# A hybrid decoder layer: moved waits at the stage borders, and head norms summed in fp32r on split squares

## The reference, cut to what matters

```python
def _rmsnorm(x, g):
    y = xf * lax.rsqrt(jnp.mean(xf * xf, axis=-1, keepdims=True) + EPS)
    return (y * g.astype(jnp.float32)).astype(x.dtype)
...
x = x + 0.5 * _swiglu(_rmsnorm(x, ffn1_norm[l]), ffn1_w_gu[l], ffn1_w_down[l])
h = _rmsnorm(x, mix_norm[l])
proj = h @ w_in[l]                       # q,k,v (stick-breaking), q,k,v (dilated), q (memory), gates
o_sb = _stick_breaking(q_sb, k_sb, v_sb)                 # 6 heads of 64
qd = _rmsnorm(q_d.reshape(B, S, N_DIL_HEADS, HEAD_DIM), dil_q_gain[l]) * scale
kd = _rmsnorm(k_d.reshape(B, S, N_DIL_HEADS, HEAD_DIM), dil_k_gain[l])
o_dil = _dilated_attention(qd, kd, v_d, rel_bias)
o_x = _memory_attention(qx, mk, mv)                      # 4 heads, 256 memory tokens
merged = g0 * (o_sb @ w_br_sb) + g1 * (o_dil @ w_br_dil) + g2 * (o_x @ w_br_x)
x = x + merged @ w_out[l]
x = x + 0.5 * _swiglu(_rmsnorm(x, ffn2_norm[l]), ffn2_w_gu[l], ffn2_w_down[l])
```

## Time and profile before

| | |
|---|---|
| three runs, median | 2374.99 us (2374.26 to 2375.61) |
| the profiled execution | 2375.41 us, span of the trace 2373.6 us |
| TensorE busy | 2331.7 us (98%) |
| VectorE busy | 1127.6 us (48%) |
| ScalarE busy | 612.1 us (26%) |
| GpSimd busy | 66.0 us (3%) |
| mean granted clock of TensorE | 0.995 |

### The profile page before, as it was taken

The page is one execution under the profiler, slowest core; times in us unless marked ns, Lnnn a source line. Parts: engine busy times, 40 slices in busy tenths (PEclk is TensorE's granted clock), DMA queues, the critical chain, the costliest instruction groups (busy, mean ns, idle before and its releaser), DMA issues.

```text
span 2373.6 us, 25801 instructions
## 1 busy us (share of the span) xinstructions
PE 2331.7 (98%) x10664; PEld 1869.5 (79%) x10664; DVE 1127.6 (48%) x1118; ACT 612.1 (26%) x787; POOL 66.0 (3%) x47
## 2 busy tenths in 40 slices
PE   8999999999999999989999999999999999999998
PEld 6888888888887766667677888878888888888887
DVE  8443444344346567755535333355444444444334
ACT  6211111111113567745344111133111111111111
POOL 2000000000002000010000000011000000000000
PEclk9999999999999999999999999999999999999999
DMA  5211111111111300110122111131111111111112
GB/s 159 75 45 53 44 53 36 53 53 44 53 47 57 115 18 18 27 42 30 29 26 63 54 45 54 54 115 37 62 51 47 51 46 49 40 53 49 49 53 71
DMA packets 47424, 125.78 MB, mean 53 GB/s; under 512 B 4285, under 2 KB 20829, under 8 KB 47104
## 3 DMA queue, kind: packets, MB, share of 16 engines
q1 hardware_dynamic: 45776, 112.69, 15.7%
q10 hardware_dynamic: 624, 10.03, 1.1%
q0 software_dynamic: 960, 2.15, 0.5%
HBM read 116.42 MB, written 9.87 MB: 53 GB/s over the span
## 4 chain that ended last, share of the span: by engine, by line
PE 92%; DVE 5%; ACT 2%; issue 1%; DMA 0%; SPq 0%; ACTq 0%; DVEq 0%
PE ps L1434 90%; DVE h_lo L920 1%; DVE w_lo L913 0%; PE ps L1914 0%; PE ps L1849 0%; DVE d_qk L1036 0%; DVE xT L982 0%; DVE x_p L1161 0%; PE ps L2005 0%; DVE pr_x L1057 0%; DMA x_nat<-in_x 0%; DVE d_qk L1060 0%; ACT pr_x L649 0%; DVE xT L1097 0%; DVE h_lo L1360 0%
## 5 line engine op out<-in xcount | busy, mean ns | idle before, releaser
L1434 PE MATMUL ps<-h_hi,w_hi 128*128 128x512 f32 x2240 | 879.5, 397 | 6.1 <-ACT h_hi L876 2.1
L1434 PE MATMUL ps<-h_lo,w_hi 128*128 128x512 f32 x2240 | 863.5, 390 | 0.2 <-DVE h_lo L920 0.2
L1434 PE MATMUL ps<-h_hi,w_lo 128*128 128x512 f32 x2240 | 701.0, 390 | 0.0
L1434 PEld LDWEIGHTS ps<-h_hi,w_hi 128*128 128x128 f32 x2240 | 420.8, 188 | 128.0 <-issue 38.9
L1434 PEld LDWEIGHTS ps<-h_hi,w_lo 128*128 128x128 f32 x2240 | 421.6, 188 | 89.6 <-DVE w_lo L913 0.4
L1434 PEld LDWEIGHTS ps<-h_lo,w_hi 128*128 128x128 f32 x2240 | 421.6, 188 | 86.8 <-issue 1.9
L576 ACT ACTIVATE w_hi<-raw 128x1024 fp32r<-128x1024 f32 x196 | 204.2, 1051 | 797.3 <-PE ps L1434 778.4
L913 DVE TENSOR_TENSOR w_lo<-raw,w_hi 128x1024 fp32r<-128x1024 f32 x196 | 249.2, 1279 | 159.6 <-ACT w_hi L576 150.1
L982 DVE TENSOR_TENSOR xT<-xT,ps 128x1024 f32<-128x1024 f32 x175 | 213.4, 1219 | 179.7 <-PE ps L1434 179.7
L1434 PE MATMUL ps<-a_hi,w_hi 128*128 128x512 f32 x704 | 275.7, 392 | 5.7 <-DVE w_lo L913 4.9
L1434 PE MATMUL ps<-a_lo,w_hi 128*128 128x512 f32 x704 | 274.7, 390 | 0.0
(11 more groups left out here) (199 smaller groups left out, 1512.9 us busy)
## 6 DMA issues: line engine op xcount, KB each, us to landing
raw<-in_weights SPq DMA_DIRECT2D x196, 512.0 KB, 3.5
x_nat<-in_x SPq DMA_DIRECT2D x8, 512.0 KB, 7.4
...
```

Of the source, the lines that this page charges most:

```text
L1434: return pe.matmul(o, a, b, start=start, stop=stop, skip_group_check=True)
```

## The change

At the start, x tile 0 is loaded, transposed and split in two halves of 512 positions, and the loads of the identity, the gains and the bias table go to other queues. Before stick-breaking, projection 6 goes to its own PSUM pair and the first scores are issued ahead of the transposes of v. In the late steps `xq_scale` follows `beside_copy`, and the scores of memory quarter 0 follow the last `sb_within`. In the memory stage the head sum of the six norm projections is made in four fp32r products of a rounded square `sq_hi` (ScalarE) and a rest `sq_lo` (GpSimd), behind two more product rows of the projection; `x_divide` is made one round earlier; on ScalarE "keep" is separated from `proj_rstd`, with `x_exp` between. Ahead of dilated attention the first scores and a fill go before the last transposes. Several PSUM pairs are exchanged.

```diff
 def proj_pair(n):
-    return 2 if n < PR_SB else n % 2 if n < PR_DIL else 2 + (n - PR_DIL) % 2
+    return 2 if n < PR_SB else n - PR_SB if n < PR_SB + 2 else 3 if n < PR_DIL else 2 + (n - PR_DIL) % 2
...
         def _(sp):
-            sp.dma_start(rel[0:32, :], rel_bias).then_inc(rel_in, 16)
-            sp.dma_start(ident, consts[:, 0, :]).then_inc(ident_in, 16)
-            sp.dma_start(g_raw[:], gains).then_inc(gain_in, 16)
-            for k in range(DT):
+            sp.dma_start(x_nat[:, 0, 0:4], x[0:512, 0:P].rearrange("(b p) c -> p b c", p=P)).then_inc(x0_in, 16)
+            sp.dma_start(raw[:, 0, :], weights[0]).then_inc(raw_in[0], 16)
+            sp.dma_start(x_nat[:, 0, 4:8], x[512:S, 0:P].rearrange("(b p) c -> p b c", p=P)).then_inc(x_in[0], 16)
+            for k in range(1, DT):
...
+            def square_split(i):
+
+                pool.wait_ge(pr_sq_done, 2 + i + 1)
+                pool.wait_ge(pr_sq_hi_done, i + 1)
+                nc.gpsimd.tensor_tensor(sq_lo[:], pr_x[0][:], sq_hi[:].bitcast(F32), ALU.subtract).then_inc(pr_sq_split, 1)
...
                     nc.scalar.activation(pr_sq[:, 0:w], proj_dest(n), ACT.Square).then_inc(pr_sq_done, 1)
+                    if n >= PR_DIL:
+                        nc.scalar.activation(sq_hi[:], proj_dest(n), ACT.Square).then_inc(pr_sq_hi_done, 1)
...
                 if n:
-                    proj_rstd(p - 1)
+                    proj_keep(p - 1)
                 if n + 1 < 8:
                     x_exp(n + 1)
+                if n:
+                    proj_rstd(p - 1)
...
-                if xq_at(s - 1) is not None:
-                    xq_scale(xq_at(s - 1))
...
                 if half_done(s) is not None:
                     beside_copy(half_done(s))
+                if xq_at(s - 1) in (0, 1, 2):
+                    xq_scale(xq_at(s - 1))
...
                 if n < 8:
-                    x_divide(n)
-                if n < 8:
                     split_lo(proj_unit(p) + AHEAD)
+                if n == 0:
+                    xq_scale(3)
                 if n + 1 < 8:
                     x_lowest(n + 1)
-                if n:
+                    x_divide(n + 1)
+                if 0 < n < 8:
                     proj_final(p - 1)
...
+                if kind == "norm" and n >= PR_DIL:
+                    pe.wait_ge(head_ready, 1)
+                    pe.wait_ge(pr_sq_split, kept_before(n) + 1)
+                    for c in (0, 512):
+                        mm(ps[:, to, c:c + 512], head_r[:], sq_hi[:, c:c + 512], True, False)
+                        last = mm(ps[:, to, c:c + 512], head_r[:], sq_lo[:, c:c + 512], False, True)
+                    last.then_inc(pr_aux, 1)
+                    return
...
-                beside(s, early, 4)
-                if s + 1 == SB_STEPS:
-
-                    pe.wait_ge(xq_final, 1)
-                    pe.wait_ge(xq_kept, 4)
-                    x_scores(0)
+                if s:
+                    beside(s, early, 4)
+                else:
+                    pe.wait_ge(pr_final, aux_before(PR_DIL))
                 sb_within(s)
+            pe.wait_ge(xq_kept, 4)
+            x_scores(0)
+            v_turn(2 * BESIDE - 1)
...
+                proj(PR_DIL + n, hh, hl, k0=DT // 2, k1=DT - 2)
                 if n:
                     proj_aux(PR_DIL + n - 1)
-                if n < 7:
-                    proj(PR_DIL + n, hh, hl, k0=DT // 2)
-                    x_values(n)
-                else:
-                    proj(PR_DIL + n, hh, hl, k0=DT // 2, k1=DT - 2)
-                    x_values(n)
-                    proj(PR_DIL + n, hh, hl, k0=DT - 2)
-
-            pe.wait_ge(xa_o, 8)
+                x_values(n)
+                proj(PR_DIL + n, hh, hl, k0=DT - 2)
+
+            pe.wait_ge(xa_exp, 32)
             pe.wait_ge(pr_final, aux_before(PR_DIL + 6))
             d_scores(0)
-            proj_aux(PR_DIL + 7)
...
-            pe.wait_ge(pr_final, aux_before(len(PROJ)))
+            pe.wait_ge(pr_final, aux_before(PR_DIL + 7))
+            fill(0)
+            proj_aux(PR_DIL + 7)
+            pe.wait_ge(xa_o, 8)
             for n in range(DN):
```

More of the change, by code:

```diff
@@ L276, in layer @@
         pr_x = [at(f"pr_x{i}", AR + (56 + 4 * i) * K, [P, S]) for i in range(3)]
+        sq_hi, sq_lo = at("sq_hi", AR + 12 * K, [P, S], F32R), at("sq_lo", AR + 56 * K, [P, S], F32R)
+        head_r = at("head_r", AR + 32 * K, [P, P], F32R)
         o_sb = at("o_sb", AR, [P, 3, S])
@@ L550, in _ @@
                     pool.dma_start(bias[:, hh, c:c + w], src).then_inc(bias_in[hh], 16)
+            for i in range(6):
+                square_split(i)
             pool.wait_ge(d_exp, DN // 2)
@@ L813, in _ @@
                 p = PR_DIL + n
+                if n == 1:
+                    act.wait_ge(xq_final, 4)
                 if n:
@@ L1271, in _ @@
                     beside_copy(half_done(s))
+                if xq_at(s - 1) in (0, 1, 2):
+                    xq_scale(xq_at(s - 1))
             sb_add(SB_STEPS - 1)
             x_lowest(0)
+            dve.wait_ge(sb_z, SB_STEPS)
+            nc.vector.tensor_copy(head_r[:], head_ones).then_inc(head_ready, 1)
             v_out(2 * BESIDE - 1)
+            x_divide(0)
             sb_out(SB_STEPS - 1)
@@ L1423, in _ @@
                     dve.wait_ge(unit_done, U_OUT + m + 1)
-                nc.vector.tensor_tensor(xT[:, m, :], x_back[:, m, :], ps[:, 2 + m % 2, :], ALU.add).then_inc(x_added, 1)
+                nc.vector.tensor_tensor(xT[:, m, :], x_back[:, m, :], ps[:, 3 - m % 2, :], ALU.add).then_inc(x_added, 1)
             for k in range(5, DT):
@@ L1593, in proj @@
                     if n < PR_DIL:
-                        after(pe, pr_copied, n if n < PR_SB else n - 1)
+                        if n == PR_DIL - 1:
+                            pe.wait_ge(newton, 4)
+                        else:
+                            after(pe, pr_copied, n if n < PR_SB else n - 1)
                     else:
@@ L1628, in proj_aux @@
                     last.then_inc(pr_aux, 1)
-            def projections(n0, n1, hi, lo):
-                for n in range(n0, n1):
-                    proj(n, hi, lo)
-                    if n == n0:
-                        norm_sum(1)
-                    else:
-                        proj_aux(n - 1)
-                proj_aux(n1 - 1)
             def turn_x(k):
@@ L1648, in _ @@
             pe.wait_ge(ident_in, 16)
-            turn_x(0)
-            turn_x(1)
+            pe.wait_ge(x0_in, 16)
+            for b in range(4):
+                last = pe.transpose(ps[:, 2, b * P:(b + 1) * P], x_nat[:, 0, b, :], ident)
+            last.then_inc(x0_turned, 1)
+            pe.wait_ge(x_in[0], 16)
+            for b in range(4, 8):
+                last = pe.transpose(ps[:, 2, b * P:(b + 1) * P], x_nat[:, 0, b, :], ident)
+            last.then_inc(x_turned, 1)
+            pe.wait_ge(hi_done, 1)
+            pe.wait_ge(h0_hi_done, 1)
+            mm(ps[:, 0, 0:512], w_hi[:, 0, 0, :], h_hi[:, 0, 0:512], True, False)
             for k in range(DT):
@@ L1818, in _ @@
             pe.wait_ge(tri_ready, 3)
+            pe.wait_ge(pr_copied, PR_SB + 2)
             sb_scores(0)
             sb_scores(1)
+            proj_aux(PR_SB + 2)
+            beside(0, 0, 4)
             for s in range(SB_STEPS):
@@ L1925, in d_values @@
                         r = head * HD
-                        last = mm(ps[r:r + HD, 2, i * P:(i + 1) * P], v_dil(g)[:, kb, r:r + HD],
+                        last = mm(ps[r:r + HD, 3, i * P:(i + 1) * P], v_dil(g)[:, kb, r:r + HD],
                                   d_pT[:, (n + head) % 3, j * P:(j + 1) * P], j == 0, j == len(held) - 1)
@@ L1991, in _ @@
                 if m == 0:
-                    last = streamed(2, u % NW, mg_hi_done, mg_split, 0)
+                    last = streamed(3, u % NW, mg_hi_done, mg_split, 0)
                 else:
-                    last = product(2 + m % 2, u % NW, hh, hl, S, read=out_read if m == DT - 1 else None)
+                    last = product(3 - m % 2, u % NW, hh, hl, S, read=out_read if m == DT - 1 else None)
                 last.then_inc(unit_done, 1)
```

59 lines of the change are left out of this document (39 added, 20 removed).

## The result

The changed kernel takes 2387.8 us (median of five runs, 2386.5 to 2390.7), the kernel before 2374.3 us on the same chip. The ratio is 1.0056, with a 95% interval of 1.0044 to 1.0068: slower by 13.5 us, where 2369.4, 5 us faster, was forecast. The profiled execution took 2390.7 us, with a span of 2388.9; it is the longest of the five and lies 2.9 above the median.

The account below looks back on a forecast made before the run. The prediction took TensorE (98% busy) to bound nearly everything. Its terms summed to +6.0 us gained, so 2375.4 - 6.0 = 2369.4 us, with a range of 2363 to 2376.

Parts of the forecast that it names:

- start: At the kernel's start, x loaded first in its queue could bring tile 0's transposes ahead; little gained, +0.3 us.
- ahead of stick-breaking: Between projection 6 and stick-breaking, first scores and beside(0) fill TensorE's waits, with a new wait of 1.0; +5.2 us.
- late stick-breaking and into memory: Late steps: xq_scale behind beside_copy delays sb_values, -1.5 us; entering memory attention: two waits go, two product rows come, +0.8.
- rest of stage: Memory stage after the last head sum: products, the sum and a wait no longer fall in it; +4.3 us.
- into dilated attention: Entry to dilated attention: first scores and a fill cover the copy, at full clock; +7.6 us, +3.2 if the clock falls.
- all behind it: Behind the entry to dilated attention: merge_pair and the output pairs change no work; 0.
- the six sums: Memory stage: the chain through GpSimd's subtraction binds, five rounds take 91.2 us in place of 83.0; -8.2 us.
- clock in this stage: Memory stage: the clock falls at three of five TensorE waits at the sum, 0.8 us each; -2.5 us.
- Rival B: Memory stage: the clock falls at all five waits, 6.2 us in place of 2.5; 2374 us, no change; chance 0.16.
- rival C: Memory stage: a clock fall lasts after each of five waits, TensorE's round of 20.5 binds; 2382 us, slower; chance 0.09.

Follow-up runs that it names:

- the o_x experiment: Changed kernel with VectorE's o_x copy put right behind x_divide, ahead of proj_final: 2372.6 us, ratio 0.9989 to the kernel before.
- the three edits: Changed kernel with o_x copy ahead of proj_final, tile 1 turned ahead of the first product, and xq_scale ahead of beside_copy: 2367.7 us, ratio 0.9972 to before.
- the sum ahead: Changed kernel with the head sum put back ahead of the two product rows, o_x copy left late: 2372.8 us, ratio 0.9990 to the kernel before.
- the one with waits of 1.0 to 1.5: Changed kernel with o_x copy early, tile 1 turned first, xq_scale ahead of beside_copy, and proj_copy ahead of proj_final: 2359.9 us, ratio 0.9935 to before.
- The experiment: Changed kernel with the transposes of x tile 1 ahead of the first product again: 2384.6 us, ratio 1.0038 to the kernel before.
- o_x early and fp32 sums: Changed kernel with o_x copy ahead of proj_final and head sums in plain fp32 of the unsplit square: 2359.3 us, ratio 0.9932 to the kernel before.
- xq_scale ahead: Changed kernel with xq_scale(0..2) ahead of beside_copy again in late stick-breaking: 2382.4 us, ratio 1.0033 to the kernel before.

## Why the prediction was wrong

By its own terms, + is gained, in the profiled executions:

| term | predicted | measured | from |
|---|---|---|---|
| start | +0.3 | -1.9 | first sum of squares 43.4 to 45.3 |
| ahead of stick-breaking | +5.2 | +5.3 | sb_values(0) at 813.80, 817.24 in the earlier trace rows, less the start |
| late stick-breaking and into memory | -1.5 +0.8 | -4.6 | first head sum at 1070.62, 1069.47 in the earlier trace rows |
| six sums and clock | -8.2 -2.5 | -18.5 | last head sum at 1172.12, 1152.42 before |
| rest of stage | +4.3 | -0.9 | copy at 1196.42, 1175.82 in the earlier trace rows |
| into dilated attention | +7.6 | +6.7 | scores at 1202.85, 1188.98 in the earlier trace rows |
| all behind it | 0 | -1.4 | end of the span |
| sum | +6.0 | -15.3 | spans: 2373.6 to 2388.9 |

The last head sum of the kernel before:

```profile
1152.42 1.98 PE L1434 MATMUL ps<-pr_x,cst 128*128 128x512 f32 x4
```

**The step that failed is "the six sums", and with it its "clock in this stage".** The prediction followed one wait, that of the sum for GpSimd, and found a true loop of 18.4: the o_x experiment shows it, to a tenth in four rounds of five and to 0.2 in the fifth. But it said of that loop "it is closed" and stopped. It didn't ask who else waits on the engines that the loop makes late. `x_turn(n)` waits for `xa_o`, the copy of quarter n-1; the copy always stood behind `proj_copy`, and `proj_copy` behind `proj_final`. Before, the scaling began 6.5 us after its sum started; with `x_exp` ahead of the root it begins 7.2 after, and with the sum behind two product rows (2.8 us) the whole train comes later against the round. Then it closes a second loop, x_turn to x_turn, over TensorE's scores and rows. At full clock that one is 18.9 (20.4 less 1.5), only 0.5 longer than the one named. It decided, because it is the longer one and because of where its wait stands. The six sums cost 18.5 us in place of 10.7.

**The clock.** Three falls of five, 2.5 us, were counted; there were six of six. Five of them cost the rounds 5 x 1.5, which is 7.5 of the 10.3 by which the five rounds (101.5 from sum to sum) exceed the predicted 91.2; the other 2.8 are the longer loop, 0.5 to 0.6 a round. The prediction held that a fall behind the wait at the sum costs 0.8, since TensorE's slack hides most; here the wait stood ahead of work that is itself on the loop, and each fall came in full. Where the wait does stand at the sum, the term was rather too high: a fall that began there made a round 0.6 us longer (18.98 in the three edits and 18.94 with the sum ahead, for 18.4) or 0.3 (17.78 for 17.53), and one that began over 1 us behind the sum made it no longer. The rest of the stage is the sixth such wait: 3.5 and 1.5 for its clock are 5.0 of the 5.2 that separate -0.9 from +4.3. With the o_x edit and its companions it goes: from the last sum to the scores of the table's sixth row pass 25.6 us with the three edits together (1152.61 to 1178.16), 30.7 in the changed kernel.

Rival B ("the clock falls at all five waits") had this part right, though not its place or its price (2374). The Trainium skill's "TensorE: Matmul & The Clock Gate", "HAM oscillation", describes a kernel whose waits throttle the clock at every tile. The changed kernel's six waits of 2.8 to 3.5 agree (0.54 to 0.59 behind each). The runs with waits at the sum agree only in part: the clock fell behind two of five in three kernels (waits of 0.8 to 3.0) and behind none in the one with waits of 1.0 to 1.5.

The prediction's list of cases for B was also short: it has "none after one of 2.45", which is the wait near 2340, but in the same trace the clock fell behind another wait of 2.45, for w_lo near 741 (0.72 from 740 to 746).

**Start.** Mis-sized and of the wrong sign: 0.5 lost on average (five kernels at 43.7 to 44.1 against 43.4), 1.9 in the profiled execution, where x landed late as well. Tile 1's transposes stand behind a product that itself waits for the first tile's halves, so its copy on VectorE came at 13.30 and not at 11.38 as before; "they end where they do now" was false. The experiment gives 1.2 to 1.5 back.

**Ahead of stick-breaking** was right in size, mechanism and in the new wait (1.07 for a forecast 1.0). **Into dilated attention** was right but for two small waits (0.75 for d_st and 0.2 for the copy), 0.9 in all.

**Late stick-breaking.** The waits came as predicted, above 2 us at `sb_values` of step 31 (2.54 for 2.5). Of the -4.6, 3.0 belong to the profiled execution. Its clock fell behind the wait of 1.70 near 997 too (0.71 from 997.4 to 1000.9) and stayed down for 6.8 us from 1016 on. The kernels with the sum ahead and with o_x early don't differ up to there, and show one fall of 3.4 us; from the wait for w_lo near 741 to `x_turn` of quarter 0 they take 305.8 and 305.9 us, the changed kernel 308.9. -1.6 against -0.7 is the usual size. With o_x early and fp32 sums no fall at all followed the wait of 2.55 (1.00 from 1000 to 1030).

**All behind it.** A wait of 2.05 for `h_hi`, at 1574 in the changed kernel and at 1535 to 1578 in the others, stands in all. Behind it the clock fell in the changed kernel (0.72 from 1574 to 1578) and in nine of the eleven experiments; it stayed full in the kernel before (1.00 from 1560.7 to 1564.1), with xq_scale ahead and with o_x early and fp32 sums. That one fall is about the -1.4. It varies with no edit near it, and its cause stays open.

The chances: slower had 0.09, all on rival C, in which a fall lasts. In the memory stage none lasted: each took 3.4 us. The loss came from a mechanism that was not on the list, and the forecast's share of 0.56 rested on one loop followed with care and no search for another.
